# A running minimum as the exponential's bias, and score pieces of two subtiles in turn

## The chip, the core and the metric

The kernel runs on one core of a Trainium2 chip. The metric is the time of one execution in microseconds (us), lower is better. Three runs of the kernel before took 3363.97, 3369.36 and 3369.91 us, so the median is 3369.36 us. TensorE multiplies matrices, VectorE works elementwise and reduces, ScalarE applies functions such as the exponential, GpSimd does smaller elementwise work, and SyncE issues most transfers. Each engine works through its own queue in order; between engines there are semaphores.

## What is computed

The program is two transformer blocks over 2048 tokens of width 1024. The first block has two full attentions side by side: an eight-head causal attention with queries and keys of 96 elements (here called `mla`), and an eight-head attention with heads of 64 (`dsa`), whose mask an index stage has chosen beforehand (at most 256 keys for each query). The second block has an attention in a narrow band, which the change doesn't touch. Cut to what matters:

```python
sc = jnp.einsum('bqhd,bkhd->bhqk', qb, kb_).astype(jnp.float32) * scale   # scale = 96 ** -0.5, dsa: 64 ** -0.5
sc = jnp.where(causal, sc, -jnp.inf)                                      # dsa: where(valid, sc, -inf)
p = jax.nn.softmax(sc, axis=-1).astype(v.dtype)
o = jnp.einsum('bhqk,bkhd->bqhd', p, v)
```

Queries and keys are normed with a gain (`mla_q_gain`, `dsa_q_gain`), and turned by their positions, before this.

## The kernel before

The program is a row of stages: a front (norms and projections), the first attention, the index stage with the gates, the second attention, the merge, the banded attention and the final projection. Both long attentions run through one function, `stage_attention`.

**Units and subtiles.** A unit is a block of rows that shares its keys' and values' work. It has four subtiles of 128 queries. In the first attention a unit is one head and a group g of 512 queries (32 units), and subtile s has 128 * (4g + s + 1) keys. Even heads go through g = 0, 1, 2, 3, and odd heads through 3, 2, 1, 0. In the second one a unit is a tile of 128 queries t and one of two key heads, the four subtiles are the four query heads that share it, and all have 128 * (t + 1) keys (32 units, two for each t). Below, an "n-block unit" is one with n = t + 1 blocks of 128 keys.

**Score pieces (`S` steps).** The scores of a subtile are made in pieces of at most 512 keys, so one to four pieces for each subtile. TensorE writes a piece into one of three PSUM banks (`p_s`; three matmuls of high and low halves in the first attention, two in the second). VectorE moves it to SBUF (`probs`), adds the mask, and takes the maximum over the piece in the same instruction (line 1059). That instruction is a `CUSTOM_DVE_ANT_0` in the trace, with a `DVE_READ_ACCUMULATOR2_ANT` behind it for the maximum. At a subtile's last piece VectorE reduces the up to four maxima to one (line 1077), and multiplies it with minus the scale (line 1081); the product is `shift`.

**Exponentials (`E` steps).** ScalarE computes exp(scale * x + shift) over a whole subtile (line 1124), 128 to 2048 elements wide, and sums it up on the way. In the queue of steps an `E` stands behind the first `S` step after its subtile's last piece; that of the fourth subtile stands at the end of the unit's round.

**Transposing and weighing (`B` and `V` steps).** For each block of 128 keys TensorE transposes the four subtiles' probabilities into one of three other PSUM banks (`p_t`, line 1029). ScalarE copies it out as the high half (`th`, line 1132), VectorE subtracts for the low half (`tl`, line 1089), and TensorE multiplies both halves with the values three blocks later (lines 993 and 995). `V` transposes the inverse sums (line 1041), which ScalarE copies as `spread` (line 1139), and `O` scales the output.

**The order.** `schedule` writes the steps of all engines in one list. A round n holds the `S` and `E` steps of unit n and the `B` and `V` steps of unit n - 1: first up to eight `S` steps (the lead), and then the `B` steps with the remaining `S` steps spread over them. The first `B` step waits for all four exponentials of its own unit, the fourth `B` step for the bank that the first has filled. With one piece for each subtile a unit has 4 `S` steps, with four 16, so units of one or two pieces for each subtile have all of theirs in the lead.

**Front.** GpSimd multiplies queries and keys with their gains (`gains`, lines 705 to 715), one tile of 128 tokens after the other.

## Time and profile before

| | |
|---|---|
| runs | 3363.97, 3369.36, 3369.91 us |
| span of the profiled execution | 3364.2 us |
| TensorE, VectorE, ScalarE, GpSimd busy | 93%, 62%, 54%, 23% of the span |
| first attention | about 441 to 941 us |
| second attention | about 1600 to 2061 us |

The span is from the first to the last instruction of one profiled execution. For that execution no other time than its span is given; the median of the three runs is 5.2 us above it. A busy TensorE is not TensorE at its peak, as matmuls are pipelined and their ends are modelled. So the share of 93% says little about small gaps: where TensorE stands still for less than a matmul's modelled end, the waits view doesn't show it, and the distance from start to start in the timeline does. Idle time of ScalarE or VectorE costs something only where TensorE comes to wait for it.

### The profile page before, as it was taken

What the parts mean: (1) busy time and instruction counts of PE and PEld (TensorE: products, weight loads), DVE (VectorE), ACT (ScalarE), POOL (GpSimd) and SP (SyncE); (2) the same over time, 40 slices, a digit from 0 to 9 for tenths busy, and PEclk for the clock granted to TensorE, in tenths of its full rate; (3) what the DMA queues carried; (4) which work ended last, traced back from release to release, by engine and by line L of the source; (5) the groups of instructions that cost most, each with busy time, mean ns of one, the idle gap of its engine ahead of it and who ended that gap; (6) DMA issues with size and microseconds to landing.
All of it is one profiled execution on the core that took longest, in us unless ns stands there. A gap on an engine that the chain in (4) does not pass through costs nothing. (4 is left out here: it accounts for less than half of the span.)

```text
span 3364.2 us, 51229 instructions
## 1 busy us (share of the span) xinstructions
PE 3143.6 (93%) x17304; PEld 2640.8 (78%) x17304; DVE 2081.7 (62%) x5125; ACT 1821.8 (54%) x3613; POOL 770.7 (23%) x1075
## 2 busy tenths in 40 slices
PE   7999879999979999997899997999989999979998
PEld 6888768888868877776667776999878888869997
DVE  6767768888845666654899886534446666642112
ACT  6565556677756766664777775211246666642121
POOL 6444401111112122222211001101034444321110
PEclk9999989999989999999999999999999999979999
DMA  5666664436152222224511103534532222143342
GB/s 176 202 203 195 200 140 96 90 71 142 57 197 79 75 84 79 77 84 115 150 44 31 31 20 99 176 123 136 173 119 74 74 67 63 56 154 128 123 126 75
DMA packets 307188, 370.46 MB, mean 110 GB/s; under 512 B 24800, under 2 KB 251936, under 8 KB 303088
## 3 DMA queue, kind: packets, MB, share of 16 engines
q1 hardware_dynamic: 293728, 320.77, 33.0%
q0 software_dynamic: 13200, 46.42, 4.3%
q8 instruction: 139, 2.28, 0.3%
q14 instruction: 121, 0.99, 0.1%
HBM read 216.32 MB, written 150.80 MB: 109 GB/s over the span
## 5 line engine op out<-in xcount | busy, mean ns | idle before, releaser
L93 PE MATMUL i_p_g<-i_hT_lo,i_wh 128*128 128x512 f32 x768 | 308.4, 401 | 9.8 <-DVE i_wl L1647 9.8
L95 PE MATMUL i_p_g<-i_hT_hi,i_wh 128*128 128x512 f32 x768 | 306.0, 398 | 0.0
L94 PE MATMUL i_p_g<-i_hT_hi,i_wl 128*128 128x512 f32 x768 | 305.8, 398 | 0.0
L1665 DVE SCALAR_TENSOR_TENSOR i_score<-i_relu,i_w,i_score 128x1024 f32<-128x1024 f32 (+7 forms) x154 | 155.1, 1024 | 167.8 <-ACT i_relu L1550 165.8
L1560 ACT ACTIVATE i_above<-i_score,i_less 128x2048 bf16<-128x2048 f32 (+13 forms) x140 | 183.2, 1308 | 106.4 <-POOL i_less L1617 70.1
L1089 DVE TENSOR_TENSOR mla_tl<-mla_p_t,mla_th 128x512 fp32r<-128x512 f32 (+1 forms) x320 | 185.8, 605 | 44.8 <-ACT mla_th L1132 42.7
L1132 ACT ACTIVATE mla_th<-mla_p_t 128x512 fp32r<-128x512 f32 (+1 forms) x320 | 163.8, 529 | 87.1 <-PE mla_p_t L1029 84.6
L1089 DVE TENSOR_TENSOR dsa_tl<-dsa_p_t,dsa_th 128x512 fp32r<-128x512 f32 x272 | 179.7, 685 | 37.7 <-ACT dsa_th L1132 32.3
L1059 DVE CUSTOM_DVE_ANT_0 dsa_probs<-dsa_p_s,dsa_mask 128x512 f32<-128x512 f32 (+3 forms) x320 | 184.4, 604 | 17.4 <-PE dsa_p_s L1814 15.1
L1132 ACT ACTIVATE dsa_th<-dsa_p_t 128x512 fp32r<-128x512 f32 x272 | 154.9, 592 | 66.0 <-PE dsa_p_t L1029 65.1
L1550 ACT ACTIVATE i_relu<-i_p_s 128x1024 f32<-128x1024 f32 (+7 forms) x176 | 141.6, 813 | 77.4 <-DVE i_score L1662 39.3
L1029 PE MATMUL mla_p_t<-ident,mla_probs 128*128 128x128 f32 x1088 | 172.7, 274 | 11.2 <-DVE mla_tl L1089 9.8
L93 PEld LDWEIGHTS i_p_g<-i_hT_lo,i_wh 128*128 128x128 f32 x768 | 146.1, 190 | 45.3 <-issue 10.2
L1124 ACT ACTIVATE dsa_probs<-dsa_probs,dsa_shift 128x128 f32<-128x128 f32 (+15 forms) x128 | 153.9, 1202 | 43.7 <-DVE dsa_shift L1081 43.2
L1124 ACT ACTIVATE mla_probs<-mla_probs,mla_shift 128x1280 f32<-128x1280 f32 (+15 forms) x128 | 153.6, 1201 | 40.5 <-DVE mla_shift L1081 39.0
L95 PEld LDWEIGHTS i_p_g<-i_hT_hi,i_wh 128*128 128x128 f32 x768 | 145.7, 190 | 35.2
L1029 PE MATMUL dsa_p_t<-ident,dsa_probs 128*128 128x128 f32 x1088 | 166.7, 276 | 6.0 <-ACT dsa_probs L1124 2.7
L94 PEld LDWEIGHTS i_p_g<-i_hT_hi,i_wl 128*128 128x128 f32 x768 | 146.1, 190 | 31.2
L1029 PEld LDWEIGHTS mla_p_t<-ident,mla_probs 128*128 128x128 f32 x1088 | 133.3, 140 | 47.3 <-DVE mla_tl L1089 17.4
L1029 PEld LDWEIGHTS dsa_p_t<-ident,dsa_probs 128*128 128x128 f32 x1088 | 131.6, 141 | 49.2 <-DVE dsa_tl L1089 19.7
L93 PE MATMUL b_p_p<-b_wl,b_xh 128*128 128x512 f32 (+1 forms) x384 | 162.1, 422 | 8.6 <-DVE b_wl L596 8.6
L93 PE MATMUL win_p_p<-win_wl,win_xh 128*128 128x512 f32 x384 | 165.2, 430 | 1.5 <-DVE win_xl L2338 1.5
(341 smaller groups left out, 9665.0 us busy)
## 6 DMA issues: line engine op xcount, KB each, us to landing
scratch_gates<-i_ob SPq DMA_DIRECT2D x95, 256.0 KB, 2.4
m_m<-scratch_gates SPq DMA_DIRECT2D x64, 256.0 KB, 3.9
f_hs<-scratch_h2T SPq DMA_DIRECT2D x16, 1024.0 KB, 9.2
scratch_qkT<-b_th SPq DMA_DIRECT2D x64, 192.0 KB, 2.6
scratch_qkT<-b_tl SPq DMA_DIRECT2D x64, 192.0 KB, 3.0
i_ws<-in_w_in SPq DMA_DIRECT2D x24, 512.0 KB, 4.9
b_xt<-in_x SPq DMA_DIRECT2D x16, 512.0 KB, 4.8
scratch_h<-b_xh POOLq DMA_DIRECT2D x16, 512.0 KB, 3.0
```

Source lines behind the costliest of these rows:

```text
L93: pe.matmul(out, l[0], r[1], start=start, stop=False)
L94: pe.matmul(out, l[1], r[0], start=False, stop=False)
L95: return pe.matmul(out, l[0], r[0], start=False, stop=stop)
L1029: last = nc.tensor.transpose(p_t[:, ring(n, place), s * P:(s + 1) * P], probs[n % R][:, s, j * P:(j + 1) * P], ident[:])
L1059: nc.vector.tensor_tensor_reduce(out=probs[n % R][:, s, k0:k0 + w], in0=p_s[:, i % A, 0:w], in1=layer.bias(n, s, k0, w), scale=1.0, scalar ...
L1089: nc.vector.tensor_tensor(tl[:, b % S, s0 * P:GT], p_t[:, ring(n, place), s0 * P:GT], th[:, b % S, s0 * P:GT].bitcast(F32), ALU.subtract). ...
L1124: nc.scalar.activation(x, x, ACT.Exp, bias=shift[:, n % R, s:s + 1], scale=layer.scale, accum_out=sums[:, n % R, s:s + 1]).then_inc(exped, 1)
L1132: nc.scalar.activation(th[:, b % S, s0 * P:GT], p_t[:, ring(n, place), s0 * P:GT], ACT.Copy).then_inc(hi_done, 1)
L1550: nc.scalar.activation(relu[:, n % 3, 0:width], p_s[:, n % 2, 0:width], ACT.Relu).then_inc(relued, 1)
L1560: nc.scalar.activation(above[:, 0:keys], score[:, x % 2, 0:keys], ACT.Sign, bias=less[:, x % 2:x % 2 + 1], accum_out=signs[:, i % 2:i % 2 ...
L1665: nc.vector.scalar_tensor_tensor(out=acc, in0=r, scalar=w[:, t, h:h + 1], in1=acc, op0=ALU.mult, op1=ALU.add).then_inc(summed, 1)
```

## The change

There are three parts. The piece instruction takes the minimum, starting from the minimum of the same subtile's piece before it (`so_far`, an operand in SBUF), so that the last piece's result covers the subtile. The query gains are multiplied with minus the scale once, so that scores come out negated and scaled; the exponential becomes exp(-x + least), and the mask's fill changes its sign. With these the reduction and the multiplication (lines 1077 and 1081) and the semaphore `shifted` are gone. And score pieces of subtiles 0 and 1, then of 2 and 3, stand in turn (`score_steps`).

```diff
@@ gains (front, GpSimd)
                 if t == 0:
                     pool.wait_ge(const_in, 16 * 5)
+                    g.tensor_scalar(qk_gain[:, 0], qk_gain[:, 0], -QK ** -0.5, None, ALU.mult)
+                    g.tensor_scalar(b_gain[:, 0], b_gain[:, 0], -HD ** -0.5, None, ALU.mult)
+                    pool.drain()
@@ schedule
+MOST = 3e38
+
+def score_steps(n, unit, paired):
+    pieces = [[("S", n, s, c, k0, min(GT, keys - k0), k0 + GT >= keys) for c, k0 in enumerate(range(0, keys, GT))]
+              for s, keys in enumerate(unit["keys"])]
+    if not paired:
+        return [step for sub in pieces for step in sub]
+    return [step for first in (0, 2) for pair in zip(pieces[first], pieces[first + 1]) for step in pair]
...
-            pending = []
-            if step[6] and not batched:
-                pending = [("E", n, step[2])]
-            elif step[6] and step[2] == 3:
-                pending = [("E", n, s) for s in range(4)]
+            pending = [("E", n, step[2])] if step[6] else []
@@ stage_attention, VectorE
                     dve.wait_ge(scored, i + 1)
+                    so_far = MOST
+                    if ch:
+                        dve.wait_ge(moved, piece[n, s, ch - 1] + 1)
+                        so_far = least[:, n % R, s, ch - 1:ch]
                     nc.vector.tensor_tensor_reduce(
                         out=probs[n % R][:, s, k0:k0 + w], in0=p_s[:, i % A, 0:w],
-                        in1=layer.bias(n, s, k0, w), scale=1.0, scalar=layer.least_max(n, s),
-                        op0=ALU.add, op1=ALU.max, accum_out=maxes[:, n % R, s, ch:ch + 1]).then_inc(moved, 1)
+                        in1=layer.bias(n, s, k0, w), scale=1.0, scalar=so_far,
+                        op0=ALU.add, op1=ALU.min, accum_out=least[:, n % R, s, ch:ch + 1]).then_inc(moved, 1)
                     i += 1
...
-                    elif last:
-                        m = maxes[:, n % R, s, 0:1]
-                        dve.wait_ge(moved, i)
-                        if ch > 0:
-                            m = top[:, n % R, s:s + 1]
-                            nc.vector.tensor_reduce(m, maxes[:, n % R, s, 0:ch + 1], AX.X, ALU.max)
-                            dve.drain()
-                        if n >= R:
-                            dve.wait_ge(exped, n_sub(n - R, s) + 1)
-                        nc.vector.tensor_scalar(shift[:, n % R, s:s + 1], m, -layer.scale, None,
-                                                ALU.mult).then_inc(shifted, 1)
@@ stage_attention, ScalarE
-                    act.wait_ge(shifted, n + 1 if layer.batched else n_sub(n, s) + 1)
+                    ch = last_piece(n, s)
+                    act.wait_ge(moved, piece[n, s, ch] + 1)
                     x = probs[n % R][:, s, 0:units[n]["keys"][s]]
-                    layer.act_sub(act, n, s, shift[:, n % R, s:s + 1])
                     if n >= R and s == 0:
                         act.wait_ge(inverted, n - R + 1)
-                    nc.scalar.activation(x, x, ACT.Exp, bias=shift[:, n % R, s:s + 1], scale=layer.scale,
+                    nc.scalar.activation(x, x, ACT.Exp, bias=least[:, n % R, s, ch:ch + 1], scale=-1.0,
                                          accum_out=sums[:, n % R, s:s + 1]).then_inc(exped, 1)
@@ masks of both attentions
-                        compare_op=ALU.is_ge, fill=NEG, base=0, pattern=[[-1, P]],
+                        compare_op=ALU.is_ge, fill=-NEG, base=0, pattern=[[-1, P]],
...
-                    nc.vector.tensor_scalar(bias[:, 0:keys], s, NEG / 2, NEG, ALU.is_ge,
+                    nc.vector.tensor_scalar(bias[:, 0:keys], s, NEG / 2, -NEG, ALU.is_ge,
```

On VectorE, at the start of the round of a 14-block unit of the second attention (second key head), the queue before is this; `ISA dsa_probs...` is the piece instruction, `ISA dsa_maxes` its read of the maximum.

```order
L1059 ISA dsa_probs_21393,dsa_maxes<-dsa_p_s,dsa_mask 128x512
L1059 ISA dsa_maxes 128x1
L1059 ISA dsa_probs_21393,dsa_maxes<-dsa_p_s,dsa_mask 128x256
L1059 ISA dsa_maxes 128x1
L1077 TENSOR_REDUCE dsa_top<-dsa_maxes 128x1
L1081 TENSOR_SCALAR dsa_shift<-dsa_top 128x1
L1059 ISA dsa_probs_21393,dsa_maxes<-dsa_p_s,dsa_mask 128x512
```

These are the third and fourth piece of the first subtile, the reduction and the multiplication, and the first piece of the second subtile. In the changed kernel the third and fourth pieces of the first two subtiles stand together, with the minimum so far as a further input:

```order
L1061 ISA dsa_probs_21018,dsa_least<-dsa_p_s,dsa_mask,dsa_least 128x512
L1061 ISA dsa_least 128x1
L1061 ISA dsa_probs_21018,dsa_least<-dsa_p_s,dsa_mask,dsa_least 128x512
L1061 ISA dsa_least 128x1
L1061 ISA dsa_probs_21018,dsa_least<-dsa_p_s,dsa_mask,dsa_least 128x256
L1061 ISA dsa_least 128x1
L1061 ISA dsa_probs_21018,dsa_least<-dsa_p_s,dsa_mask,dsa_least 128x256
L1061 ISA dsa_least 128x1
L1072 TENSOR_TENSOR dsa_tl<-dsa_p_t,dsa_th 128x512
```

The first subtile's last piece has moved from fourth to seventh place of the lead, and no small instruction stands between pieces. On ScalarE, the same round before (the first line is the exponential of the unit before's fourth subtile):

```order
L1124 ACTIVATE dsa_probs_21392,dsa_sums<-dsa_probs_21392,dsa_shift 128x1792
L1124 ACTIVATE dsa_probs_21393,dsa_sums<-dsa_probs_21393,dsa_shift 128x1792
L1132 ACTIVATE dsa_th<-dsa_p_t 128x512
L1124 ACTIVATE dsa_probs_21393,dsa_sums<-dsa_probs_21393,dsa_shift 128x1792
L1132 ACTIVATE dsa_th<-dsa_p_t 128x512 x7
L1124 ACTIVATE dsa_probs_21393,dsa_sums<-dsa_probs_21393,dsa_shift 128x1792
L1132 ACTIVATE dsa_th<-dsa_p_t 128x512 x6
L1139 ACTIVATE dsa_spread<-dsa_p_t 128x512
```

And in the changed kernel:

```order
L1106 ACTIVATE dsa_probs_21017,dsa_sums<-dsa_probs_21017,dsa_least 128x1792
L1106 ACTIVATE dsa_probs_21018,dsa_sums<-dsa_probs_21018,dsa_least 128x1792
L1114 ACTIVATE dsa_th<-dsa_p_t 128x512
L1106 ACTIVATE dsa_probs_21018,dsa_sums<-dsa_probs_21018,dsa_least 128x1792
L1114 ACTIVATE dsa_th<-dsa_p_t 128x512 x13
L1106 ACTIVATE dsa_probs_21018,dsa_sums<-dsa_probs_21018,dsa_least 128x1792
L1121 ACTIVATE dsa_spread<-dsa_p_t 128x512
```

The first two exponentials keep their places among the copies. The third has moved from the middle of the round to its end, behind the thirteenth further copy.

## Rows read from the trace of the kernel before

**Rows 1.** Windows view: stretch, length, busy time by engine (PE to POOL), clock, DMA, GB/s.
```profile
441.30:941.20 499.90, 475.57 (x2816) 398.12 (x2816) 410.50 (x1260) 340.58 (x610) 62.87 (x71) 0.98 0.42 96
1600.40:2060.80 460.40, 427.58 (x2400) 327.17 (x2400) 403.70 (x1200) 332.00 (x561) 58.47 (x62) 0.99 0.20 50
```

**Rows 2.** Waits view, second attention: engine, line, releaser, us, times, longest.
```profile
PEld dsa_p_s L1813 <- DVE dsa_maxes L1059: 58.5, 115, 1.3
PEld dsa_p_t L1029 <- DVE dsa_tl L1089: 19.7, 46, 1.4
PE dsa_p_s L1813 <- DVE dsa_maxes L1059: 19.1, 51, 0.9
```

**Rows 3.** Waits view of the first attention.
```profile
PEld mla_p_t L1029 <- DVE mla_tl L1089: 17.4, 32, 1.1
```

**Rows 4.** Groups by line, VectorE, second attention: count, busy us, mean ns, idle before.
```profile
L1077 DVE TENSOR_REDUCE dsa_top<-dsa_maxes 128x1 f32<-128x2 f32 (+2 forms) x96 | 15.0, 156 | 3.3
L1081 DVE TENSOR_SCALAR dsa_shift<-dsa_top 128x1 f32<-128x1 f32 x96 | 14.8, 154 | 7.4
L1081 DVE TENSOR_SCALAR dsa_shift<-dsa_maxes 128x1 f32<-128x1 f32 x32 | 4.9, 154 | 1.1
```

**Rows 5.** Timeline of VectorE, a 14-block unit: start us, length us, instruction.
```profile
1904.01 0.69 DVE L1059 CUSTOM_DVE_ANT_0 dsa_probs<-dsa_p_s,dsa_mask 128x512 f32<-128x512 f32 x1
1904.62 0.08 DVE L1059 DVE_READ_ACCUMULATOR2_ANT dsa_maxes<- 128x1 f32 x1
...
1905.84 0.42 DVE L1059 CUSTOM_DVE_ANT_0 dsa_probs<-dsa_p_s,dsa_mask 128x256 f32<-128x256 f32 x1
1906.19 0.08 DVE L1059 DVE_READ_ACCUMULATOR2_ANT dsa_maxes<- 128x1 f32 x1
1906.31 0.16 DVE L1077 TENSOR_REDUCE dsa_top<-dsa_maxes 128x1 f32<-128x4 f32 x1
...
1906.68 0.69 DVE L1059 CUSTOM_DVE_ANT_0 dsa_probs<-dsa_p_s,dsa_mask 128x512 f32<-128x512 f32 x1
```

**Rows 6.** Timeline of TensorE, the same unit.
```profile
1903.09 0.40 PE L1814 MATMUL dsa_p_s<-dsa_k_lo,dsa_q 128*128 128x512 f32 x1
...
1907.78 0.60 PE L1029 MATMUL dsa_p_t<-ident,dsa_probs 128*128 128x128 f32 x4
...
1912.80 0.60 PE L1029 MATMUL dsa_p_t<-ident,dsa_probs 128*128 128x128 f32 x4
```

**Rows 7.** Timeline of ScalarE, the same unit.
```profile
1906.73 1.79 ACT L1124 ACTIVATE dsa_probs<-dsa_probs,dsa_shift 128x1792 f32<-128x1792 f32 x1 [0.93 <-DVE dsa_shift L1081]
...
1908.52 0.58 ACT L1132 ACTIVATE dsa_th<-dsa_p_t 128x512 fp32r<-128x512 f32 x1
1909.41 1.79 ACT L1124 ACTIVATE dsa_probs<-dsa_probs,dsa_shift 128x1792 f32<-128x1792 f32 x1 [0.31 <-DVE dsa_shift L1081]
...
1911.20 1.55 ACT L1132 ACTIVATE dsa_th<-dsa_p_t 128x512 fp32r<-128x512 f32 x3
```

**Rows 8.** Timeline of ScalarE, a 3-block unit of the second attention.
```profile
1626.74 1.55 ACT L1132 ACTIVATE dsa_th<-dsa_p_t 128x512 fp32r<-128x512 f32 x3
```

**Rows 9.** Timelines of ScalarE and TensorE, a 5-block unit.
```profile
1657.87 1.06 ACT L1132 ACTIVATE dsa_th<-dsa_p_t 128x512 fp32r<-128x512 f32 x2
...
1656.71 0.62 PE L1029 MATMUL dsa_p_t<-ident,dsa_probs 128*128 128x128 f32 x4
```

**Rows 10.** Timeline of TensorE, an 11-block unit.
```profile
1816.58 0.66 PE L1029 MATMUL dsa_p_t<-ident,dsa_probs 128*128 128x128 f32 x4
```

**Rows 11.** Timeline of TensorE, the last unit of the second attention.
```profile
2044.05 0.66 PE L1029 MATMUL dsa_p_t<-ident,dsa_probs 128*128 128x128 f32 x4 [2.67 <-ACT dsa_probs L1124]
```

**Rows 12.** Timeline of TensorE, a unit of the first attention.
```profile
888.29 0.66 PE L1029 MATMUL mla_p_t<-ident,mla_probs 128*128 128x128 f32 x4 [0.48 <-DVE mla_tl L1089]
```

**Rows 13.** Groups by line and shape, VectorE, the stage between the attentions.
```profile
L1718 DVE TENSOR_SCALAR i_taken<-i_steps,i_left 128x8 f32<-128x8 f32 x25 | 5.4, 215 | 0.0
L1722 DVE TENSOR_SCALAR i_gone<-i_taken 128x8 f32<-128x8 f32 x25 | 4.1, 165 | 0.0
```

More of the change, by code:

```diff
@@ L842 @@
     packed = True
-    batched = False
+    paired = True
     depth = 2
@@ L851, in wait_bias @@
     def wait_bias(self, dve, n, s): ...
-    def act_sub(self, act, n, s, shift): ...
-    def shift_made(self, dve, n, shift): ...
-    def add_sinks(self, dve, n, sums): ...
     def place_probs(self, space, r):
@@ L860, in sync_end, with schedule @@
     def sync_end(self, sp): ...
-    def least_max(self, n, s):
-        return -3e38
-def schedule(units, behind, lead, output_late, batched):
+MOST = 3e38
[5 more added lines that the diff above has]
+    return [step for first in (0, 2) for pair in zip(pieces[first], pieces[first + 1]) for step in pair]
+def schedule(units, behind, lead, output_late, paired):
     steps, late = [], []
@@ L875, in schedule @@
         m = n - behind
-        s_steps = []
-        if n < len(units):
-            for s in range(4):
-                keys = units[n]["keys"][s]
-                for c, k0 in enumerate(range(0, keys, GT)):
-                    s_steps.append(("S", n, s, c, k0, min(GT, keys - k0), k0 + GT >= keys))
+        s_steps = score_steps(n, units[n], paired) if n < len(units) else []
         b_steps = [("B", m, i, j, s0) for i, (j, s0) in enumerate(units[m]["blocks"])] + [("V", m)] if m >= 0 else []
@@ L920, in stage_attention @@
     R, S = layer.depth, layer.split_ring
-    steps = schedule(units, R - 1, layer.lead, layer.output_late,
-                     layer.batched)
+    steps = schedule(units, R - 1, layer.lead, layer.output_late, layer.paired)
+    piece = {step[1:4]: i for i, step in enumerate(step for step in steps if step[0] == "S")}
+    last_piece = lambda n, s: -(-units[n]["keys"][s] // GT) - 1
     n_b = [sum(len(u["blocks"]) for u in units[:n]) for n in range(len(units) + 1)]
@@ L944, in stage_attention @@
         p_o = c.enter_context(nc.psum_tensor(f"{tag}_p_o", [P, 2, GT], F32))
-        scored, moved, shifted, exped, turned, hi_done, lo_done, multiplied, inverted, inv_turned, spread_done, weighed, out_done = (
-            sem(f"{tag}_{n}") for n in ("scored", "moved", "shifted", "exped", "turned", "hi_done",
+        scored, moved, exped, turned, hi_done, lo_done, multiplied, inverted, inv_turned, spread_done, weighed, out_done = (
+            sem(f"{tag}_{n}") for n in ("scored", "moved", "exped", "turned", "hi_done",
                                         "lo_done", "multiplied", "inverted", "inv_turned", "spread_done",
@@ L1093, in _ @@
                         dve.wait_ge(exped, n_sub(n, 3) + 1)
-                        layer.add_sinks(dve, n, sums[:, n % R])
                         if n >= 2:
@@ L1159 @@
 class Mla(Attention):
-    scale = QK ** -0.5
     tag = "mla"
```

15 lines of the change are left out of this document (2 added, 13 removed).

## The prediction

> **What bounds the kernel now.** The windows view gives the lengths of both attentions, 499.9 and 460.4 us, and in each the share of every engine [rows 1]. In the first, TensorE is busy 475.6 of 499.9 us and VectorE 410.5; in the second 427.6 of 460.4, and VectorE 403.7, which is 88%. Next the waits view. In the second attention the weight loads of the scores wait 58.5 us, 115 times, for VectorE to give back a score bank, and the matmuls themselves 19.1 us; behind that come 19.7 us before the transposes, for the low half [rows 2]. In the first the greatest such wait is 17.4 us before the transposes [rows 3], as three matmuls a piece make TensorE slower than VectorE there. So the first attention is TensorE's, and the second is TensorE's with a stretch at each round's start, the lead of eight score pieces, in which VectorE sets the pace. Last the timelines of single rounds, for what a shorter lead runs into.
>
> **What is removed.** 96 reductions and 128 multiplications in each attention: 15.0 + 14.8 + 4.9 = 34.7 us busy and 3.3 + 7.4 + 1.1 = 11.8 us idle before them in the second [rows 4], together 46.5 us of VectorE. In a row: a read of the maximum starts at 1906.19, and the next piece starts at 1906.68 and not at once, so 0.49 us for a subtile there; between other pieces there is no gap (from 1904.01 to 1904.62, 0.61 us a piece of 512; 0.35 us for 256) [rows 5]. If TensorE stood still for VectorE all the time, two attentions would give back 93 us. They don't, since in most of a round VectorE waits itself for the high half.
>
> **What a shorter lead gives, and what takes it back.** Take the round of a 14-block unit. The lead's first wide piece is scored by 1903.49 (a matmul from 1903.09, 0.40 long) [rows 6]. VectorE could start it at 1903.55 and does at 1904.01 [rows 5], as the unit before's reduction is still in front. After the change it starts at 1903.55. The eighth piece needs the bank of the fifth, so TensorE begins it at 1903.55 + 5 x 0.61 + 0.15 = 1906.75, and the first transposes at about 1907.1; before they began at 1907.78 [rows 6]. That is 0.7 us gained. But the first subtile's last piece is now the seventh: it is moved at 1903.55 + 6 x 0.61 + 0.35 = 1907.56. The first exponential, which began at 1906.73 [rows 7], begins at 1907.6. It takes 1.79 us, so the first copy of a high half is at 1909.4 (before 1908.52), 0.55 us later comes the second exponential at 1909.95 (before 1909.41), and the second copy at 1911.75 (before 1911.20) [rows 7]. The fifth block's transposes need the bank whose low half follows that copy, by 0.60 for the copy, 0.69 for the subtraction and some 0.13 to hand over: 1913.17, against 1912.80 [rows 6]. So the 0.7 us are gone, and 0.37 us are lost. Behind that point TensorE has no gap in the rest of the round before or after, so what holds there holds for the round.
>
> The same working for the other widths of the second attention, always against the place where TensorE next waits for the high or low half:
> - One piece for each subtile (1 to 4 blocks, 8 units). The order doesn't change. The exponentials wait for the multiplication, with pieces 0.72 us apart; without it 0.49 to 0.60. The copy at 1626.74 [rows 8] comes at about 1626.3. -0.45 us a unit, -3.6.
> - Two pieces (5 to 8 blocks, 8 units). The first transposes at 1656.71 and the first copy at 1657.87 [rows 9] move up 0.9 and 0.7 us at 5 blocks, since two reductions in front of the fifth piece go, and 0.5 at 8 blocks. With the pointer's price below, -0.5 a unit, -4.0.
> - Three pieces (9 to 12 blocks, 8 units). Both exponentials come back to back, but the first subtile's last piece is only two places later. The fourth block's transposes, at 1816.58 in an 11-block unit [rows 10], come 0.3 us earlier. -2.4.
> - Four pieces (13 to 16 blocks, 8 units): +0.4 for 13 and 14 blocks as above; for 16, where the two removed reductions are fully on the lead, nearly nothing. With the pointer's price +0.45, +3.6.
> - The end of the stage. TensorE waits 2.67 us before the last unit's first transposes for the fourth exponential [rows 11]. The third now stands directly ahead of it, with two short copies between, and delays it by about 0.9 us. +0.9.
>
> Together -5.5 us in the second attention.
>
> **The first attention.** Its lead isn't VectorE's, as the three matmuls of a wide piece take 0.69 us and VectorE 0.61. Where g = 1 (8 units), short pieces make VectorE late, and some 0.3 us go: -2.4. Where g = 2 follows g = 3 (4 units), the fifth transposes wait 0.48 us for a low half, and a reduction and multiplication stand ahead of that on VectorE [rows 12]: -0.45 each, -1.8. There the third exponential now comes in front of the narrow last blocks, which TensorE does in 0.4 to 0.7 us and ScalarE gets only after 1.5 us: +0.5 each, +2.0. Where g = 3 follows g = 3 (4 units), two exponentials of up to 1.8 us come together: +0.4 each, +1.6. Sum -0.6.
>
> **The minimum so far as an operand.** 192 pieces in each attention read it from SBUF. Their own rows show only the constant. The nearest rows are two small VectorE instructions of the same width, one with such an operand (215 ns) and one without (165 ns) [rows 13]. I take 0.05 us a piece, and 0 as the other end; nothing in it could make a piece shorter. It counts only in the lead, 4 to 6 pieces a round, and is in the sums above. A minimum costs what a maximum does. The new wait on `moved` is for a piece two places back, done 0.6 us earlier, so it holds nobody; in its queue there would be all later pieces and low halves. Waiting on one's direct predecessor costs 0.12 us (1906.19 to 1906.31) [rows 5], and the pairing avoids just this.
>
> **The rest.** GpSimd's two further multiplications come once, on 96 and 64 elements. No row shows them; VectorE's smallest instructions take 0.16 us [rows 4], and at three times that both cost 1 us if nothing hid them. The work of the tile in which they stand is used a dozen steps later, so I take 0. Fills of another sign cost nothing. Transfers don't move: SyncE waits for the same counts of pieces and blocks.
>
> **Sum.** -5.5 - 0.6 = -6.1 us against the span of 3364.2 us, so a span of about 3358. Taken off the median of the runs, 3369.36, it gives 3363 us.
>
> **A page's rule on each side.** In the trace ScalarE is busy 332.0 of 460.4 us and still lets TensorE wait at the round's start [rows 1, 7]. The Trainium skill ("Perfetto Trace Analysis", Optimizing Scalar/DVE Operations) says that where ScalarE or VectorE isn't saturated but makes others wait, splitting instructions lets work be done sooner. The change bunches them, which is the side of the second rival. The Trainium skill ("VectorE: DVE Perf Modes", Rules for kernel authors) says to reduce the count of VectorE's instructions and not of semaphores. The change does that, and the first rival is what it would bring; the trace agrees in that 0.49 us go with two instructions of 0.16 and 0.15 us.
>
> **Rivals.**
> 1. *The lead's gain is kept.* If the copies' three banks and the three blocks' lag absorb the two exponentials, what counts is the lead: 0.7 us in the round above, and up to 1.3 us where two reductions fall into the first five pieces. 24 units by 1.2 are 29 us, with the narrow units 33 us: about 3337 us. For it speaks that 58.5 us of the weight loads' waits name VectorE's score banks [rows 2]; against it the chain of copies in the row above, which has no slack before the fifth block.
> 2. *ScalarE's pair becomes the bound, slower.* The second exponential starts when the first ends, and the fourth to sixth blocks wait for their copies. I found 0.37 us lost in one round with a start that is 0.46 us earlier. If VectorE doesn't start that earlier, or the pair holds back TensorE in the 16 wide units of the first attention too, each of the 32 units with three or four pieces loses 0.6 to 0.9 us: +24, less 8 for the narrow units and 2.4 for g = 1, so +13 us or 3383 us. It decides from the point where the fifth block's transposes wait longer than the lead has become shorter.
> 3. *It changes nothing.* What VectorE saves is idle time of VectorE elsewhere: 3369 us.
>
> **How the numbers follow.** A measurement of this kernel can tell about 0.2%, 6.7 us, from no change. The forecast is at the edge of it: 50%, with its own range of 3356 to 3370, of which a bit under half is faster by more than 0.2%, and the rest within. Rival 1 has 22%, all faster. Rival 2 has 20%, of which 18 are slower by more than 0.2%. Rival 3 has 8%, nearly all within. Faster 0.45, within 0.35, slower 0.20. The range reaches from most of rival 1, 3340 us, to most of rival 2, 3380 us.
>
> **What will show it.** In the profile after, VectorE's busy time is about 35 us smaller in each attention, and pieces follow at 0.61 to 0.66 us. The waits of the scores' weight loads for VectorE in the second attention fall to under half of 58.5 us. The waits of transposes for the low half rise above 19.7 us. In the 14-block round the first exponential begins about 4 us behind the first wide piece's start on VectorE, the fifth transposes later than before relative to the round's start. The second attention is 5 us shorter, the first the same. I am wrong if the second attention is shorter by more than 15 us (the copies had slack), if it is longer, or if pieces with the operand take over 0.75 us.

## The result, and the profile after

The changed kernel takes 3376.24 us (median of 7 runs, 3375.34 to 3379.74), the kernel before 3369.36 (7 runs beside it, 3363.97 to 3371.07). The ratio is 1.0025 with a 95% interval of 1.0015 to 1.0034: 0.25% slower, where I had forecast 3363.

The windows view of the changed kernel, both attentions in the order and columns of [rows 1]:

```profile
442.00:954.00 512.00, 481.27 (x2820) 403.29 (x2821) 394.78 (x1036) 335.33 (x610) 62.84 (x71) 0.98 0.41 95
1606.20:2071.10 464.90, 430.29 (x2400) 327.47 (x2400) 379.31 (x976) 325.79 (x561) 58.46 (x62) 0.99 0.19 49
```

The reader is to see two things that go against each other. VectorE has 224 instructions less in each attention and is 15.7 and 24.4 us less busy, so that part of the change does what it says. And both stretches are longer, by 12.1 and 4.5 us, at the same mean granted clock. (The first window ends 1.6 us behind the next stage's first matmul, at 952.39; before it ended at that matmul, 941.31. From start to that matmul the first attention is 10.4 us longer. The profiled spans differ by 10.3 us, 3374.5 against 3364.2, since the stage between the attentions is 5.9 us shorter: 663.2 against 669.1 from TensorE's last instruction of the first attention to its first of the second. In the nine experiments, whose work there is the same, it was between 664.6 and 670.2. It scatters, and is left out of what follows.)

The waits view of the second attention names what became longer (columns as in [rows 2]). The first line is from the kernel before, the others from the changed one:

```profile
ACT dsa_probs L1124 <- DVE dsa_shift L1081: 43.2, 74, 1.2
...
DVE dsa_tl L1072 <- ACT dsa_th L1114: 71.8, 90, 3.1
PEld dsa_p_s L1793 <- DVE dsa_least L1061: 47.6, 120, 1.3
ACT dsa_probs L1106 <- DVE dsa_least L1061: 41.3, 32, 2.9
PEld dsa_p_t L1027 <- DVE dsa_tl L1072: 35.7, 58, 1.8
PE dsa_p_t L1027 <- DVE dsa_tl L1072: 12.7, 24, 1.3
```

The scores wait less for a bank, 47.6 us for 58.5 [rows 2]. The transposes' weight loads wait 35.7 us for a low half where they waited 19.7, and the transposes themselves 12.7 (the two can overlap in time). The exponentials wait no longer in all than before, 41.3 us for 43.2, but in fewer and longer waits, up to 2.9 us for 1.2. The weight loads' wait for a low half in the first attention went from 17.4 us [rows 3] to 25.3:

```profile
ACT mla_probs L1106 <- DVE mla_least L1061: 55.7, 39, 6.3
PEld mla_p_t L1027 <- DVE mla_tl L1072: 25.3, 37, 1.6
```

Now the 14-block unit of [rows 5 to 7], on VectorE (start, length, instruction):

```profile
1907.97 0.69 DVE L1061 CUSTOM_DVE_ANT_0 dsa_probs<-dsa_p_s,dsa_mask 128x512 f32<-128x512 f32 x1
...
1909.20 0.75 DVE L1061 CUSTOM_DVE_ANT_0 dsa_probs<-dsa_p_s,dsa_mask,dsa_least 128x512 f32<-128x512 f32 x1
1909.87 0.08 DVE L1061 DVE_READ_ACCUMULATOR2_ANT dsa_least<- 128x1 f32 x1
...
1911.89 0.48 DVE L1061 CUSTOM_DVE_ANT_0 dsa_probs<-dsa_p_s,dsa_mask,dsa_least 128x256 f32<-128x256 f32 x1
1912.29 0.08 DVE L1061 DVE_READ_ACCUMULATOR2_ANT dsa_least<- 128x1 f32 x1
```

On ScalarE, with the idle time before an instruction and its releaser in brackets:

```profile
1912.40 1.80 ACT L1106 ACTIVATE dsa_probs<-dsa_probs,dsa_least 128x1792 f32<-128x1792 f32 x1 [1.72 <-DVE dsa_least L1061]
...
1914.19 0.57 ACT L1114 ACTIVATE dsa_th<-dsa_p_t 128x512 fp32r<-128x512 f32 x1
1914.67 1.78 ACT L1106 ACTIVATE dsa_probs<-dsa_probs,dsa_least 128x1792 f32<-128x1792 f32 x1
...
1916.44 1.06 ACT L1114 ACTIVATE dsa_th<-dsa_p_t 128x512 fp32r<-128x512 f32 x2
```

And on TensorE: the first wide piece's last matmul, the first transposes, and the fifth block's.

```profile
1907.40 0.40 PE L1794 MATMUL dsa_p_s<-dsa_k_lo,dsa_q 128*128 128x512 f32 x1
...
1911.69 0.60 PE L1027 MATMUL dsa_p_t<-ident,dsa_probs 128*128 128x128 f32 x4
...
1917.88 0.66 PE L1027 MATMUL dsa_p_t<-ident,dsa_probs 128*128 128x128 f32 x4 [0.68 <-DVE dsa_tl L1072]
```

Counted from the moment the first wide piece is scored (1907.80; before 1903.49), the first transposes come after 3.89 us (before 4.29), 0.40 us sooner. The first exponential comes after 4.60 us instead of 3.24, since the first subtile's last piece is now the seventh of the lead. ScalarE stands idle for 1.72 us in front of it, and the first block's copy, whose transposes begin at 1911.69, stands behind it in the queue until 1914.19; after that one copy comes the second exponential, and the next copies start at 1916.44. So the fifth transposes come after 10.08 us instead of 9.31: 0.77 us late. The lead has become shorter and the round longer.

To place this over the whole kernel I measure rounds: in TensorE's timeline, from one unit's transposes of the reciprocals (line 1041 before, 1039 after) to the next unit's, and the first round from the first score. The table gives the sum of the changes against the kernel before, in us. The columns go by the unit that is scored in the round: in the second attention by its score pieces in a subtile, then the last round, which scores none, and in the first attention by the same count (g + 1, as g runs from 0 to 3). The rows below the first are the experiments, with the median of all their runs and the ratio to the kernel before, run beside them.

```
                        second attention              first attention
                      1    2    3    4  last       1    2    3    4    all  median   ratio (95%)
change             -2.2 -3.8 +3.1 +5.3 +2.2     -0.4 +2.1 +0.5 +8.6  +15.4 3376.24  1.0025 (1.0015-1.0034)
e1 unpaired        -2.0 -4.1 -0.1 +3.5 -0.1     -0.3 -2.0 +1.4 +6.3   +2.6 3367.05  0.9995 (0.9986-1.0004)
e2 pairing only    +0.0 +4.7 +4.6 +9.0 +2.3     +0.0 +4.5 +1.8 +10.7 +37.7 3405.74  1.0116 (1.0100-1.0131)
e3 constant start  -0.9 -4.6 +1.1 +2.8 +2.1     -0.4 +1.6 -0.6 +7.4   +8.7 3370.07  1.0005 (0.9996-1.0014)
e4 reduction kept  -2.0 -5.2 -5.0 -6.6 +1.6     -0.4 -4.4 -2.7 -0.8  -25.6 3339.19  0.9909 (0.9896-0.9923)
e5 first two       -2.5 -5.2 -0.5 +6.6 +1.6     -0.4 -3.6 +0.7 +9.3   +6.1 3374.45  1.0017 (1.0008-1.0026)
e6 last two        -2.2 -1.2 -2.2 -7.5 +0.7     -0.4 -0.3 -3.2 -0.6  -16.7 3349.89  0.9942 (0.9928-0.9955)
e7 second late     -2.5 -3.8 -2.3 -3.0 +2.0     -0.4 +2.1 -1.3 +2.0   -7.1 3357.11  0.9964 (0.9950-0.9977)
e8 e4, second late -2.1 -5.2 -0.3 -7.0 +1.6     -0.4 -5.5 -0.1 -0.8  -19.7 3346.49  0.9932 (0.9918-0.9946)
e9 both late       -1.3 -3.8 +1.5 -6.2 +2.0     -0.4 +1.5 +2.2 +2.2   -2.3 3360.64  0.9980 (0.9971-0.9989)
```

Rounds are from one execution of each kernel, and two things bound what they tell. Columns with the same instructions differ by up to 1.2 us (one piece in e7 and e9; two pieces of the first attention in e4 and e8, by its first round). And the medians stand up to 8.5 us lower against the kernel before than the rounds do (the change: +6.9 for +15.4), which the rounds leave open.

### The profile page after: what moved, and what is told of

The parts are those of the page before. It is cut to its first block and busy times, and to the rows that moved or that the text cites. A ratio compares the mean times of both kernels' runs of the same rounds, so it can differ in the third digit from the quotient of the medians.

```text
span 3374.5 us, 50924 instructions
## 1 busy us (share of the span) xinstructions
PE 3147.8 (93%) x17304; PEld 2641.6 (78%) x17304; DVE 2039.2 (60%) x4677; ACT 1810.4 (54%) x3613; POOL 770.0 (23%) x1077
## 5 line engine op out<-in xcount | busy, mean ns | idle before, releaser
L1027 PE MATMUL dsa_p_t<-ident,dsa_probs 128*128 128x128 f32 x1088 | 167.7, 277 | 17.4 <-DVE dsa_tl L1072 12.7
L1106 ACT ACTIVATE mla_probs<-mla_probs,mla_least 128x1280 f32<-128x1280 f32 (+15 forms) x128 | 153.0, 1197 | 55.7 <-DVE mla_least L1061 55.7
L1027 PEld LDWEIGHTS dsa_p_t<-ident,dsa_probs 128*128 128x128 f32 x1088 | 131.3, 142 | 64.3 <-DVE dsa_tl L1072 35.7
L1027 PEld LDWEIGHTS mla_p_t<-ident,mla_probs 128*128 128x128 f32 x1088 | 133.6, 140 | 55.2 <-DVE mla_tl L1072 25.3
L1106 ACT ACTIVATE dsa_probs<-dsa_probs,dsa_least 128x128 f32<-128x128 f32 (+15 forms) x128 | 153.3, 1198 | 41.7 <-DVE dsa_least L1061 41.3
L93 PE MATMUL m_p_b<-m_ol,m_bh 128*128 128x256 f32 x512 | 147.1, 287 | 17.3 <-POOL m_ol L2699 17.3
```

What stands on the lines that cost most here:

```text
L93: pe.matmul(out, l[0], r[1], start=start, stop=False)
L1027: last = nc.tensor.transpose(p_t[:, ring(n, place), s * P:(s + 1) * P], probs[n % R][:, s, j * P:(j + 1) * P], ident[:])
L1106: nc.scalar.activation(x, x, ACT.Exp, bias=least[:, n % R, s, ch:ch + 1], scale=-1.0, accum_out=sums[:, n % R, s:s + 1]).then_inc(exped, 1)
```

## The experiments

The theory after the result: the alternating order costs more than everything else gives, because the first exponential stands at the head of ScalarE's queue and waits for a piece that has moved back. The rivals: the operand in SBUF makes the pieces dear, or the wait for the piece before does. Below, the expectations call the first theory A (A1 where the loss lies at the round's start, A2 at its end) and the rivals B.

**e1: the change without the alternating order.** The running minimum and the scale in the gains stay.

```diff
-    paired = True
+    paired = False
```

> The changed kernel with the score pieces in the old order, subtile after subtile; the running minimum, the gains and the missing reduction and multiplication stay. Theory A (the order loses the time: in pairs, the first subtile of a wide unit is complete two or three pieces later, so the first exponential and the first copies of high halves come later): the rounds with wide units lose the 0.5 to 1.35 us that they have gained in the changed kernel, and VectorE is spared 0.49 us a subtile less 0.06 us a piece for the operand and 0.12 to 0.2 us a piece for waiting on the piece directly in front; 3362 to 3367 us, so 9 to 14 us faster than the changed kernel. Rival B (the operand and the wait for it lose the time): as the wait is now on the direct predecessor, it gets slower still, 3378 us or more.

3367.05 us, no difference from before. Against the change the rounds are 12.8 us shorter, so the order is dearer than what it avoids. But e1 isn't fast either. VectorE's timeline at the same 14-block unit shows why:

```profile
1905.70 0.08 DVE L1061 DVE_READ_ACCUMULATOR2_ANT dsa_least<- 128x1 f32 x1
1905.92 0.75 DVE L1061 CUSTOM_DVE_ANT_0 dsa_probs<-dsa_p_s,dsa_mask,dsa_least 128x512 f32<-128x512 f32 x1
1906.60 0.08 DVE L1061 DVE_READ_ACCUMULATOR2_ANT dsa_least<- 128x1 f32 x1
1906.83 0.75 DVE L1061 CUSTOM_DVE_ANT_0 dsa_probs<-dsa_p_s,dsa_mask,dsa_least 128x512 f32<-128x512 f32 x1
```

A piece that waits for its direct predecessor starts 0.22 or 0.23 us after the read's start, where an independent one starts with the read. I had expected 0.12 to 0.2. With the operand's 0.06 a piece follows the other at 0.91 us instead of 0.61 [rows 5]. Four pieces of a subtile pay that three times, 0.9 us, in place of one reduction and one multiplication at 0.49 together.

**e2: the alternating order alone**, on the kernel before, with its maxima, reductions and multiplications.

```diff
-        s_steps = []
-        if n < len(units):
-            for s in range(4):
-                keys = units[n]["keys"][s]
-                for c, k0 in enumerate(range(0, keys, GT)):
-                    s_steps.append(("S", n, s, c, k0, min(GT, keys - k0), k0 + GT >= keys))
+        s_steps = score_steps(n, units[n], True) if n < len(units) else []
```

> The kernel before with the pieces of two subtiles in turn and nothing else changed: maximum, reduction and multiplication stay. Theory A: all of the order's cost without what the missing small instructions give, so 15 to 20 us slower than before, 3384 to 3390 us; first attention 10 us or more longer. Rival B: no change, 3369 us.

3405.74 us, 1.1% slower, and outside what I had expected. Nothing dear was added to VectorE here, so the cost is the order's alone: 37.7 us of rounds. That is three times the 12.8 us between e1 and the change, so the order's price isn't one number: e1's old order pays for the chain of pieces, which the alternation avoids. The waits of the second attention:

```profile
ACT dsa_probs L1128 <- DVE dsa_shift L1085: 57.0, 37, 3.0
...
PEld dsa_p_t L1033 <- DVE dsa_tl L1093: 43.3, 54, 1.8
```

The longest wait of an exponential is 3.0 us, and the transposes' weight loads wait 43.3 us for low halves, against 19.7 [rows 2].

**e3: the changed order, each piece started from the constant.** The wait for the piece before stays. The exponential takes a fixed bias of zero and a scale of -0.01, so the outputs are not the attention's; the work is the same in kind and size.

```diff
+        zero, zeroed = sb("zero", [P, 1]), sem(f"{tag}_zeroed")
...
                         dve.wait_ge(moved, piece[n, s, ch - 1] + 1)
-                        so_far = least[:, n % R, s, ch - 1:ch]
...
-                    nc.scalar.activation(x, x, ACT.Exp, bias=least[:, n % R, s, ch:ch + 1], scale=-1.0,
+                    nc.scalar.activation(x, x, ACT.Exp, bias=zero[:], scale=-1e-2,
```

> The changed kernel, but every piece's minimum starts from the constant and not from the operand in SBUF, with the wait on the earlier piece kept; the exponential takes a bias of zero and a scale of -0.01, so that the outputs are not the attention's. It prices the operand alone. Pieces of 512 that took 0.743 us take 0.686 us again. Theory A: the operand is a smaller part, four to six pieces of a lead by 0.06 us in 32 wide units, 5 to 9 us faster than the changed kernel, 3367 to 3371 us. Rival B: the operand is all of it, 3362 us or less. If nothing changes, 3376 us, the lead isn't bound by VectorE any more.

The operand's price can be read in the changed kernel's own groups by line and shape (busy us, mean ns), second attention:

```profile
L1061 DVE CUSTOM_DVE_ANT_0 dsa_probs<-dsa_p_s,dsa_mask,dsa_least 128x512 f32<-128x512 f32 x120 | 86.0, 745 | 0.0
L1061 DVE CUSTOM_DVE_ANT_0 dsa_probs<-dsa_p_s,dsa_mask 128x512 f32<-128x512 f32 x104 | 67.8, 685 | 2.9 <-PE dsa_p_s L1794 1.6
```

60 ns a piece of 512, where I took 50 by the nearest rows [rows 13]. In e3 the rounds are 6.7 us shorter than in the changed kernel, 3370.07 us in all. By medians it is 6.2 us, as expected. So the operand is a part of the loss, and the smaller one. With it gone the wide units are still longer than before (+2.8 and +7.4), which the operand rival can't explain.

**e4: old order, constant start, the reduction kept, only the multiplication gone.**

```diff
-    paired = True
+    paired = False
...
-                    so_far = MOST
-                    if ch:
-                        dve.wait_ge(moved, piece[n, s, ch - 1] + 1)
-                        so_far = least[:, n % R, s, ch - 1:ch]
...
-                        in1=layer.bias(n, s, k0, w), scale=1.0, scalar=so_far,
+                        in1=layer.bias(n, s, k0, w), scale=1.0, scalar=MOST,
...
+                    if last and ch:
+                        dve.wait_ge(moved, i)
+                        nc.vector.tensor_reduce(top[:, n % R, s:s + 1], least[:, n % R, s, 0:ch + 1],
+                                                AX.X, ALU.min).then_inc(reduced, 1)
```

> Old order, minimum started from the constant in each piece, one reduction over up to four minima kept for subtiles of several pieces, and only the multiplication gone (scale in the gains as in the changed kernel). VectorE is spared about 0.25 us a subtile in 128 subtiles of each attention, and no exponential comes later. Theory A: 3361 to 3366 us, at least as fast as before in each round. Rival B gives the same here, since there is no operand; both fall if it is slower than before.

3339.19 us, 0.9% faster than the kernel before and the fastest of all that ran. I had expected 3361 to 3366, so this missed too, and why so little VectorE time is worth so much I can't say. Against the kernel before, more than the multiplication is gone from VectorE's queue: the `drain` between reduction and multiplication, and the wait for an exponential of two units earlier. No run takes these apart. VectorE at the end of the first subtile of the 14-block unit:

```profile
1884.32 0.08 DVE L1060 DVE_READ_ACCUMULATOR2_ANT dsa_least<- 128x1 f32 x1
1884.44 0.16 DVE L1067 TENSOR_REDUCE dsa_top<-dsa_least 128x1 f32<-128x4 f32 x1
1884.56 0.69 DVE L1060 CUSTOM_DVE_ANT_0 dsa_probs<-dsa_p_s,dsa_mask 128x512 f32<-128x512 f32 x1
```

0.24 us between two pieces where it was 0.49 [rows 5]. The exponential starts at 1884.63, 2.49 us after the subtile's first piece (1882.14); before it was 2.72 [rows 5, 7], in the changed kernel 4.43. Its waits of the second attention beside those of the changed kernel:

```profile
PEld dsa_p_s L1801 <- DVE dsa_least L1060: 47.5, 115, 1.3
...
ACT dsa_probs L1114 <- DVE dsa_top L1067: 20.7, 51, 0.8
...
PEld dsa_p_t L1030 <- DVE dsa_tl L1075: 9.7, 30, 0.6
```

This rules out the score banks as what sets the change apart from e4: the scores' weight loads wait as long for one, 47.6 and 47.5 us. The exponentials wait 20.7 us, at most 0.8 at a time, and not 41.3 and 2.9; the transposes' weight loads wait 9.7 us for a low half and not 35.7. e1 less e4 is 28.2 us of rounds: so much the running minimum costs in the old order instead of one reduction. In e1 the banks do have a part in it, with 59.3 us, beside 18.3 us for low halves.

**e5 and e6: e4 with the pieces of subtiles 0 and 1 alone alternating, and of 2 and 3 alone.**

```diff
-    if not paired:
-        return [step for sub in pieces for step in sub]
-    return [step for first in (0, 2) for pair in zip(pieces[first], pieces[first + 1]) for step in pair]
+    steps = []
+    for first in (0, 2):
+        a, b = pieces[first], pieces[first + 1]
+        steps += [step for pair in zip(a, b) for step in pair] if first in paired else a + b
+    return steps
```

> The kernel with the reduction kept (constant start, no multiplication, 3339 us in old order), with only the pieces of subtiles 0 and 1 in turn. Theory A1 (the loss of pairing lies at the round's start: first exponential late, first copies late): nearly all of the loss, 15 to 22 us slower than 3339, so 3355 to 3361 us; rounds with wide units lose 0.7 to 1.3 us each, the last round of the second attention stays. Theory A2 (it lies at the round's end: third exponential late, in front of the last copies and of the fourth): under 5 us, 3344 us or less.

> The same kernel with only the pieces of subtiles 2 and 3 in turn. Theory A1: 3340 to 3345 us; the last round of the second attention, where nothing covers the exponentials, about 2 us longer. Theory A2: 3355 us or more.

e5 takes 3374.45 us (expected 3355 to 3361) and e6 3349.89 (3340 to 3345): the place was right, and its price again too low. Against e4 the rounds are 31.7 us longer with the first pair and 9.0 with the last. So the round's start is the place, and there the wide units: of the 31.7 us, 23.4 are in units with four pieces, 8.0 with three. If the two add, which no run shows, e4 with both pairs would stand at 15.1 us above the kernel before, where the change stands at 15.4. By this estimate the running minimum costs next to nothing once the order alternates, and the alternation about 41 us. e5's waits in the second attention are the changed kernel's:

```profile
ACT dsa_probs L1116 <- DVE dsa_top L1069: 47.1, 36, 2.6
...
PEld dsa_p_t L1032 <- DVE dsa_tl L1077: 36.0, 64, 1.8
```

The last pair costs 8.1 us in units with two pieces. There the lead holds all eight pieces, and the third exponential comes right before the first copies; that this is the cause I argue from the order and haven't tried apart. In units with three pieces of the second attention it costs 2.8 us. In units with four it costs nothing, so there the exponential delayed to the round's end doesn't matter.

**e7: the changed kernel with the second exponential put behind the copies of the first four blocks** in units with three or four pieces. If what counts is who stands ahead of the copies in ScalarE's queue, this must give time back with the score order as it is.

```diff
+            if pending and step[2] == 1 and step[3] > 1 and m >= 0:
+                held.extend(pending)
+                pending = []
...
+            if x == 3:
+                steps.extend(held)
+                held.clear()
```

> The changed kernel, where the second subtile's exponential stands behind the fourth block's copy in units of three or four pieces, and not behind the first's. Theory A1 with the fifth transposes as the place: the copies of blocks 2 to 4 no longer wait for it, so the wide rounds of both attentions get back what they lost against before; 10 to 16 us faster than the changed kernel, 3360 to 3366 us. If the late first exponential alone makes the loss (copy of block 1, transposes of block 4), under 4 us, 3372 us or more.

3357.11 us, a larger gain than the 3360 to 3366 us expected. The rounds are 22.5 us shorter than the change's, 28 of the 32 of wide units by 0.4 to 1.2, while the four that go from g = 1 to g = 2, and those of one and two pieces, are the same within 0.3. Nothing changed on TensorE and VectorE but what they wait for. The second attention's waits:

```profile
ACT dsa_probs L1112 <- DVE dsa_least L1067: 41.3, 32, 2.9
PEld dsa_p_t L1033 <- DVE dsa_tl L1078: 18.7, 37, 0.8
```

The first exponential waits the same 41.3 us. The transposes' weight loads wait 18.7 us for a low half and not 35.7. So of the pair it is the second exponential, 1.8 us between the first copy and the second, that made the fifth block late. e7's rounds are still 18.5 us longer than e4's. The last pair (9.0 in e6) and the operand (6.7 in e3) would be most of that if they add; the first exponential's lateness is not priced by itself.

**e8: the same on e4**, and **e9: e7 with the first exponential moved as well**, behind the second block, the second behind the fifth. The edit of e8 to e4 is that of e7; e9 against e7:

```diff
-            if pending and step[2] == 1 and step[3] > 1 and m >= 0:
+            if pending and step[2] <= 1 and step[3] > 1 and m >= 0:
...
-            if x == 3:
-                steps.extend(held)
-                held.clear()
+            if held and x in (1, 4):
+                steps.append(held.pop(0))
```

> The kernel with the reduction kept in old order, with the same later place of the second exponential. In this order the first exponential is done before the first copy is due. Theory A1: the rest of the waits for a low half at the fifth transposes goes, 3 to 8 us faster than 3339 us, 3331 to 3336 us. If there is no such wait left in old order, 3339 us.

> The changed kernel, with the first subtile's exponential behind the second block's copy and the second subtile's behind the fifth's, in units of three or four pieces (with the second alone moved behind the fourth it took 3357.1 us). In the changed kernel ScalarE stands still 1.7 to 3 us before the first exponential, with the first copy ready behind it. If this standing in the queue is what is left of the loss, the wide rounds get 0.2 to 0.6 us shorter once more: 3347 to 3353 us. If what is left is VectorE's time (the operand, 0.06 us a piece), nothing more comes back: 3356 to 3360 us.

Both missed. e8 takes 3346.49 us (0.9932, 0.9918 to 0.9946), 7 us more than e4 in medians and 5.9 in rounds. The loss is in the units with three pieces, +4.7 and +2.6. In the old order their second subtile is complete within the lead, so the exponential could run while TensorE still scored; put behind the fourth block it runs where the copies are wanted (argued from the order, not tried apart). In units with four pieces it gives only 0.4 us. e9 takes 3360.64 us (0.9980, 0.9971 to 0.9989), 3.5 us more than e7. Its rounds with 13 or 14 blocks are 0.5 to 0.7 us shorter, those with three pieces 0.3 to 0.6 longer. So neither of its two cases came: what is left of the loss isn't simply the standing in the queue. An order of ScalarE's queue that is good for one width is bad for another, and neither e7 nor e9 brought the alternating order to e4.

## Why the prediction was wrong

The mechanism was the one I named, and its sizes on the losing side were too small: it went the way of the second rival, ScalarE's pair as the bound, for which I had 3383 us and one chance in five. I forecast -6.1 us and the rounds give +15.4. Of the miss of 21.5 us, 7.0 are in the units with g = 3, where the failed step is "+0.4 each" for 4 units, and 5.5 in the second attention's units with three pieces, where it is "the first subtile's last piece is only two places later". The g = 1 units give another 4.5.

1. *One and two pieces*, -3.6 and -4.0: -2.2 and -3.8. Right, the first somewhat large. For g = 2 in the first attention, +0.2: +0.5.
2. *Three pieces*, -2.4: measured +3.1. It is two places, but I counted no cost for the pair of exponentials that then stands ahead of the copies, and the lead's gain of 0.3 us didn't come. The 11-block unit of [rows 10] shows it, first before and then after:

```profile
1807.95 0.60 PE L1041 MATMUL dsa_p_t<-ident,dsa_inv 128*128 128x128 f32 x4
1811.49 1.47 ACT L1124 ACTIVATE dsa_probs<-dsa_probs,dsa_shift 128x1408 f32<-128x1408 f32 x1 [0.86 <-DVE dsa_shift L1081]
1815.16 1.61 ACT L1132 ACTIVATE dsa_th<-dsa_p_t 128x512 fp32r<-128x512 f32 x3
...
1809.85 0.60 PE L1039 MATMUL dsa_p_t<-ident,dsa_inv 128*128 128x128 f32 x4
1814.79 1.47 ACT L1106 ACTIVATE dsa_probs<-dsa_probs,dsa_least 128x1408 f32<-128x1408 f32 x1 [2.00 <-DVE dsa_least L1061]
1816.26 1.46 ACT L1106 ACTIVATE dsa_probs<-dsa_probs,dsa_least 128x1408 f32<-128x1408 f32 x1
1817.71 1.54 ACT L1114 ACTIVATE dsa_th<-dsa_p_t 128x512 fp32r<-128x512 f32 x3
1819.14 0.65 PE L1027 MATMUL dsa_p_t<-ident,dsa_probs 128*128 128x128 f32 x4 [0.43 <-DVE dsa_tl L1072]
```

Counted from the reciprocals, the first exponential comes after 4.94 us instead of 3.54, the first copies after 7.86 instead of 7.21, and the fourth transposes after 9.29 instead of 8.63: about 0.65 us late where I had 0.3 early. e5 confirms the place: the alternation of the first two subtiles alone costs 4.5 us in these units.

3. *Four pieces*, +3.6: measured +5.3. In the 14-block unit I had 0.37 us for the fifth transposes and it is 0.77. VectorE began 0.17 us after the scoring (1907.97 against 1907.80) and not 0.06. From there the first exponential took 4.43 us, where my sum had 4.05: five of the first seven pieces are 0.06 to 0.07 us dearer, and 0.11 us lies between the last read and the exponential. My list had added 0.05 us for the operand.
4. *The last round*, +0.9: +2.2. The wait is 3.35 us for 2.67 [rows 11], so the delay of 0.7 is near the forecast. The other 1.5 us are TensorE's clock (below), of which e4 has as much without any longer wait, so that part needn't be the change's.
5. *First attention, g = 1*, -2.4: +2.1. Of this 1.4 are in the very first round, and their cause is open: that round scatters by 1.1 us between e4 and e8, which have the same steps there, and in e2, which alternates too, it is only 0.1 longer. Without it the change stands at +0.7, and e1, in the old order, at -2.7. The last pair is the likely rest: in e6, without that round, it costs 4.7 us in these units.
6. *g = 3*, +1.6 for 4 units: measured +8.6, and this is the largest miss. I had charged only units that follow a unit as wide, and 0.4 us each. The rounds show it in all eight: about 0.8 us where g = 3 follows g = 2, and 1.3 to 1.4 where it follows g = 3. From one of the first kind, reciprocals, first and fifth transposes, before and after:

```profile
713.97 0.60 PE L1041 MATMUL mla_p_t<-ident,mla_inv 128*128 128x128 f32 x4
719.32 0.60 PE L1029 MATMUL mla_p_t<-ident,mla_probs 128*128 128x128 f32 x4
724.42 0.60 PE L1029 MATMUL mla_p_t<-ident,mla_probs 128*128 128x128 f32 x4
...
720.74 0.60 PE L1039 MATMUL mla_p_t<-ident,mla_inv 128*128 128x128 f32 x4
726.06 0.60 PE L1027 MATMUL mla_p_t<-ident,mla_probs 128*128 128x128 f32 x4
731.89 0.66 PE L1027 MATMUL mla_p_t<-ident,mla_probs 128*128 128x128 f32 x4 [0.42 <-DVE mla_tl L1072]
```

The first transposes come as soon as before (5.32 us after the reciprocals for 5.35), and the fifth 0.7 us later (11.15 for 10.45). So the lead gives nothing here that the late copies could use up, and the whole delay is lost. In the other kind of unit the fifth transposes come 1.3 us later. ScalarE is late as in the second attention:

```profile
726.52 1.68 ACT L1106 ACTIVATE mla_probs<-mla_probs,mla_least 128x1664 f32<-128x1664 f32 x1 [2.99 <-DVE mla_least L1061]
```

It idles 2.99 us before the first exponential. I had written that the first attention is TensorE's and its lead not VectorE's, and taken that as cover. It was the reverse: where TensorE sets the lead's pace, there is no gain to set against an exponential that comes several pieces later, and that count of pieces is the same in both attentions.

7. *What is removed.* I costed the reduction, the multiplication and the alternation together, as one step. Taken in this order they are worth -25.6 us (multiplication, e4), +28.2 (running minimum in place of the reduction, in the old order) and +12.8 (the alternation on top of that); in another order the two losses divide otherwise, as e2, e5 and e6 show. I gave the first rival, the lead's gain kept, about 3337 us, and e4 takes 3339. The numbers meet by luck: the rival had all of its 33 us in the second attention and both small instructions gone, while e4 keeps the reduction and gains 17.3 us in the second attention and 8.3 in the first.

Of the signs that I named, the longer waits for low halves, the fifth transposes later and the operand's pieces below 0.75 us came. The second attention is longer, which I had named as a sign of being wrong. "Under half of 58.5" for the score banks didn't come (47.6), nor did 35 us less on VectorE (15.7 and 24.4). The removed 34.7 us were there, but the dearer pieces gave some back: 192 pieces at 0.06 us are 11.5 us in each attention. That leaves 23.2, which fits the second; of the first, 7.5 us aren't accounted for. Pieces with the operand followed each other at 0.67 us and not at 0.61 to 0.66. GpSimd's two further multiplications, which I took at 0, can't be seen: the first attention starts at 442.0 us for 441.3 before, and between 440.4 and 444.6 in the experiments.

The Trainium skill says that breaking up instructions may get work done sooner where ScalarE or VectorE isn't saturated but makes other engines wait ("Perfetto Trace Analysis", Optimizing Scalar/DVE Operations). No run here splits one. What e5 and e7 show is near it: bunched exponentials on an engine that is busy 70% of the stretch cost 31.7 and 22.5 us of rounds. The Trainium skill's rule to reduce the count of VectorE's instructions ("VectorE: DVE Perf Modes", Rules for kernel authors) isn't for this case: e1 has 96 fewer than e4 in each attention, in the same order, and takes 28 us more.

## What to carry to other kernels

In a queue that is served in order, ask of every reordering which instruction completes a *group* and how many places later it now comes, and then what stands behind the one that waits for it; the price is paid some blocks later, on another engine, and a shorter busy time on the reordered engine says nothing about it. A running result as an operand of the next instruction turns independent instructions into a chain; one small reduction at the end was cheaper (0.24 us a subtile against 0.9 us). When a change has parts that each work on the same stretch, run them apart: the part that paid (the scale put in the gains) was hidden under others that cost more. Their prices needn't add: the alternation cost 12.8 us on top of the chained pieces and 37.7 us by itself.

## What the runs showed of the hardware

**Waiting for one's predecessor.** On VectorE a reduction that reads the result of the piece before it starts 0.12 us after that read starts (1884.32 to 1884.44 in e4, as in [rows 5]). A piece that takes it as its scalar operand starts 0.22 or 0.23 us after (1906.60 to 1906.83 in e1), and the operand makes it 60 ns longer in either order of the pieces. With another piece between, the start isn't delayed: in the changed kernel's 14-block unit the next piece starts with the read at 1909.87, and pieces with the operand follow at 0.67 us.

**The clock after a wait.** TensorE's last round in the second attention shows something that the length of the wait doesn't explain. Windows of 5 us behind the wait for the last exponential, in the columns of [rows 1]. The kernel before, after 2.67 us idle:

```profile
2044.00:2049.00 5.00, 4.96 (x35) 4.27 (x35) 3.22 (x6) 2.99 (x5) 0.40 (x1) 1.00 0.00 0
```

e4, after 2.67 us idle too:

```profile
2018.00:2023.00 5.00, 5.00 (x25) 4.18 (x24) 2.79 (x6) 2.33 (x4) 0.38 (x1) 0.66 0.00 0
```

The changed kernel, after 3.35 us:

```profile
2052.60:2057.60 5.00, 4.96 (x23) 4.23 (x24) 1.70 (x4) 1.79 (x3) 0.00 (x0) 0.66 0.00 0
```

The granted clock stayed at 1.00 (2.4 GHz) in the first; in the other two it was 0.66 in the mean, with groups of four transposes at 1.05 us in place of 0.60, so part of the stretch at 1.2 GHz. It costs e4 1.6 us in its last round. The length of the wait doesn't decide it: after 2.67 us the transposes stayed at full speed in the kernel before and in e1, and slowed down in e4, e5 and e8; after 3.35 us they stayed at full speed in e6, whose last round is only 0.7 us longer, and slowed down in the changed kernel, e2, e3, e7 and e9. What decides isn't shown by these runs.
